# Hybrid decoder block on one core: one weight ring for three stages, adaLN columns run on, and two of eight one-hot units made by ScalarE

## Chip, cores and metric

One core of one Trainium2 chip. The metric is device microseconds of one execution, the median of the runs. Engines are named as in the profile: PE is TensorE (PEld its weight loads), DVE is VectorE, ACT is ScalarE, POOL is GpSimd, SP is SyncE, which issues most DMA transfers.

## The reference, cut to what matters

One sequence of T = 512 positions, width D = 1024, all in float32. adaLN: a vector c gives six vectors of shift, scale and gate.

```python
mod = jax.nn.silu(c) @ w_ada[l] + b_ada[l]            # 1024 x 6144
sh1, sc1, gt1, sh2, sc2, gt2 = jnp.split(mod[:, None, :], 6, axis=-1)
h = rmsnorm(x, norm_pre_mix[l]) * (1.0 + sc1) + sh1
y = token_mixer(h, ...)
x = x + gt1 * rmsnorm(y, norm_post_mix[l])
h = rmsnorm(x, norm_pre_ffn[l]) * (1.0 + sc2) + sh2
y = peer(h, w_q[l], sub_keys[l], u_tab[l], v_tab[l])
x = x + gt2 * rmsnorm(y, norm_post_ffn[l])
```

The token mixer projects h by w_in, runs a gated short convolution and a gated delta rule (q and k normed by head, chunks of 64), and merges:

```python
merged = jax.nn.sigmoid(gate_sc) * br_sc + jax.nn.sigmoid(gate_dn) * br_dn
return merged @ w_mix_out
```

peer picks 16 of 16384 experts per head and position (8 heads) with gates from a softmax, and sums over them gate × gelu(h · u) × v:

```python
act = jax.nn.gelu(jnp.einsum('btd,bted->bte', hb, u), approximate=False)
return jnp.einsum('bte,bted->btd', gb * act, vv)
```

## The kernel before

Everything runs in float32 precision on TensorE by parts: a float32 tile is split into a high part in fp32r (a copy on ScalarE, "hi") and the rest (a subtraction, "lo"), and a product is three matmuls, hi × hi, lo × hi and hi × lo. A weight tile is 128x1024 (8 blocks of 128x128, 512 KB), so each tile costs a load on SyncE's queue, a split on ScalarE of about 1.06 us, a subtraction on GpSimd of about 2.33 us, and 24 matmuls of 512 columns.

The program is a row of stages, each one block in which every engine has its own instruction stream and waits for the others by semaphores. A helper (Steps) names the counts: V, A and E are the steps of VectorE, ScalarE and TensorE, and `V.after("lo3")` is the wait for VectorE's step lo3. A stage ends when all engines have ended.

*First stage (project_stage, 0 to 180 us).* c goes through Silu into the PSUM tile `bank_pair`, the same row in all partitions. The adaLN products are made by VectorE: for each of 48 columns of w_ada, transposed to a 128x1024 tile of the ring `ada` (6 buffers), one scalar_tensor_tensor with accumulator, L428. The first 16, shift and scale of the first norm, are needed for h; the other 32 lie between later work. For x, ScalarE squares (L364) and takes the root, VectorE inverts (L437) and scales x to `xn` (L440), TensorE transposes xn (L294), ScalarE applies scale and shift (h_raw, L380) and copies the high part (h_hi, L383), and VectorE subtracts (h_lo, L452). This goes in rounds k = 0, 2, 4, 6 of four columns and two tiles of h. TensorE multiplies each h tile by w_ab (L307), and then tile n of 16 of the projection (L318), whose weights pass through `wring` (4 buffers). Behind tile 11 it sums the squares of q and k by head and spreads the inverse norm (L337), for which ScalarE takes the root of a 16x512 tile and VectorE the reciprocal (L503), both in the slot n == 10 of their loops over tiles.

*Delta stage (180 to 407 us).* The delta rule of 8 chunks, and 12 further projection tiles between its parts.

*Merge stage (merge_stage, 408 to 617 us).* It has its own tiles merge_w, merge_w_hi and merge_w_lo of two buffers. First VectorE makes a gate vector and a diagonal 128x1024 tile twice (L1102, L1104); TensorE turns each into a row that all partitions hold (L996), and ScalarE copies it out. ScalarE copies the high parts of both branches, VectorE subtracts the low ones (L1108). Then four rounds of six weight pieces (two gates and one piece of both branches' outputs, twice): L1005, with the sigmoid on ScalarE and the products and sums on VectorE. At the end eight pieces of w_mix_out, k = 0 to 7, go into all eight PSUM banks, one per output (4 blocks of positions, 2 halves), L1028; for the last two pieces both are waited for and each output takes k = 6 and 7 together. ScalarE squares each output for the norm (L1086).

*Retrieve stage (617 to 1043 us).* The queries, the choice of experts, and products h · u for some of them. Its last steps turn the experts' row and column indices and the gates of 384 positions into `idxT` and `gateT`.

*Gate stage (scatter_stage, 1043 to 1306 us).* For each of the 384 positions, a 128x128 matrix of gates over all 16384 experts is made by a product of two one-hot matrices on TensorE: `hot1` (hot_i in the trace) compares a row of numbers with the first index, for eight positions in one operation of 128x1024 (L1588), and `hot2` (gated_i) compares it with the second index and multiplies by the gate, one operation of 128x128 for each position, with two pointers (L1592):

```python
last = nc.vector.tensor_scalar(hot2[:, u % RH, t, :], C["iota"], idxT[:, 1, at], gateT[:, at], ALU.is_equal, ALU.mult)
```

There are 6 iterations of 8 units of 8 positions. A unit is eight such products (16 matmuls in the trace, L1624); ScalarE copies them out of two PSUM banks in two pieces (L1652), and they are stored. PSUM has room for two units, the one-hots have four buffers (RH = 4). In six of the eight units (0, 1, 2, 4, 5, 6) TensorE also multiplies a tile of u by h (24 matmuls of 384 columns, L1633), whose split is on ScalarE (L1642), whose low part is on VectorE (L1597), and whose Gelu is on ScalarE (L1660). VectorE has one more product of 128x1024 per unit (L1601), for the 128 positions whose experts are gathered by row instead. VectorE, TensorE and ScalarE each run a hardware loop over the iterations.

*Expert stage (1307 to 1947 us).* The products h · u that are left, the gates times gelu, and the sum over v, in 128 tiles. The change touches it only by the buffer of its v tiles.

## Time and profile before

| | us |
|---|---|
| median of 3 runs | 1945.85 (1945.83 to 1947.31) |
| the profiled execution | 1948.68 |
| its span | 1946.8 |
| PE busy | 1786.5 (92%) |
| DVE busy | 1339.8 (69%) |
| ACT busy | 701.2 (36%) |
| POOL busy | 757.5 (39%) |
| mean granted TensorE clock | 0.965 of full |

The span is from the first to the last instruction of the profiled execution, which is one of its own and not one of the three. A busy share is a mean over stages of different kinds: what matters for a change in one stage is who waits for whom in that stage. TensorE's granted clock is 1.00 or 0.50 of full speed in a short stretch (2.4 and 1.2 GHz).

### The profile page before, as it was taken

The page shows a single profiled execution, that of the slowest core. Times are in us where ns is not written, and L with a number is a line of the kernel's source. Part 1 is how long each engine was busy: PE and PEld are TensorE (multiplying, and loading weights), DVE is VectorE, ACT ScalarE, POOL GpSimd, SP SyncE. Part 2 cuts the span into 40 slices and gives each one's busy share as a digit, 9 for nine tenths or more (in the row PEclk, how much of TensorE's full clock was granted, in tenths as well). Part 3 has the DMA queues.
Part 4 walks back from the last instruction along what each step waited for, and adds up shares of the span by engine and source line. Part 5 has one row for each costly group of instructions (what it writes and reads, how often), then busy time and mean ns, then how long its engine had stood idle before and what let it go on. Part 6 is the DMA issues. An engine that isn't in the chain of part 4 may idle for free. (4 is left out here: it accounts for less than half of the span.)

```text
span 1946.8 us, 31281 instructions
## 1 busy us (share of the span) xinstructions
PE 1786.5 (92%) x11421; PEld 1570.5 (81%) x11421; DVE 1339.8 (69%) x2857; ACT 701.2 (36%) x1041; POOL 757.5 (39%) x443
## 2 busy tenths in 40 slices
PE   2899899979995998999998999979999999999997
PEld 1566777868874787999998999969998888888886
DVE  4783555543323467878776999967787888777776
ACT  3432223333314323333333445433333333333333
POOL 0332233214432345777772333313455443333330
PEclk9898999989997999999998999989999999999999
DMA  7672010013322226888885999998789999988983
GB/s 256 228 256 87 24 35 13 2 55 97 97 87 101 73 87 205 291 291 285 290 280 173 304 313 302 312 315 287 262 326 331 360 370 368 328 322 317 327 319 114
DMA packets 178681, 432.51 MB, mean 222 GB/s; under 512 B 15752, under 2 KB 91656, under 8 KB 178464
## 3 DMA queue, kind: packets, MB, share of 16 engines
q1 hardware_dynamic: 125088, 273.71, 42.1%
q0 software_dynamic: 36864, 134.23, 19.2%
q10 hardware_dynamic: 16640, 23.36, 3.3%
q8 instruction: 57, 0.93, 0.2%
q14 instruction: 32, 0.26, 0.0%
HBM read 383.54 MB, written 47.71 MB: 222 GB/s over the span
## 5 line engine op out<-in xcount | busy, mean ns | idle before, releaser
L198 POOL DMA_INDIRECT own_rows<-in_peer_v_dram,own_row x128 | 214.4, 1675 | 328.7 <-DVE y_own L1888 310.0
L1384 POOL TENSOR_TENSOR piece_lo<-v_tile,piece_hi 128x1024 fp32r<-128x1024 f32 x84 | 202.0, 2405 | 153.8 <-ACT piece_hi L1314 153.7
L198 POOL DMA_INDIRECT own_rows<-in_u_rows_dram,own_row x128 | 161.8, 1264 | 246.9 <-DVE own_rows L1601 185.4
L1245 PE MATMUL bank<-h_hi,piece_hi 128*128 128x384 f32 (+1 forms) x672 | 237.2, 353 | 13.8 <-DVE h_lo L1490 7.0
L1245 PE MATMUL bank<-h_lo,piece_hi 128*128 128x384 f32 (+1 forms) x672 | 234.9, 350 | 0.0
L1245 PE MATMUL bank<-h_hi,piece_lo 128*128 128x384 f32 (+1 forms) x672 | 234.9, 350 | 0.0
L1798 PE MATMUL bank<-v_hi,coef_lo 128*128 128x512 f32 x512 | 199.7, 390 | 0.0
L1798 PE MATMUL bank<-v_lo,coef_hi 128*128 128x512 f32 x512 | 199.6, 390 | 0.0
L1798 PE MATMUL bank<-v_hi,coef_hi 128*128 128x512 f32 x512 | 199.2, 389 | 0.1
L1314 ACT ACTIVATE piece_hi<-v_tile 128x1024 fp32r<-128x1024 f32 x84 | 89.3, 1063 | 254.2 <-PE bank L1245 244.9
L1873 DVE TENSOR_TENSOR v_lo<-v_tile,v_hi 128x1024 fp32r<-128x1024 f32 x128 | 156.5, 1223 | 24.7 <-ACT v_hi L1829 22.8
L1888 DVE SCALAR_TENSOR_TENSOR y_own<-own_rows,own_coef,y_own 128x1024 f32<-128x1024 f32 x128 | 163.8, 1280 | 1.3 <-DMA own_rows<-in_peer_v_dram,own_row 0.2
L1829 ACT ACTIVATE v_hi<-v_tile 128x1024 fp32r<-128x1024 f32 x128 | 135.0, 1055 | 48.2 <-PE bank_pair L1798 48.2
L1245 PEld LDWEIGHTS bank<-h_hi,piece_hi 128*128 128x128 f32 x672 | 127.6, 190 | 21.4 <-issue 10.7
L1833 ACT ACTIVATE coef_hi<-coef 128x384 fp32r<-128x384 f32 x128 | 67.1, 524 | 211.5 <-DVE coef L1912 211.5
L1245 PEld LDWEIGHTS bank<-h_hi,piece_lo 128*128 128x128 f32 x672 | 127.3, 189 | 6.0
L1245 PEld LDWEIGHTS bank<-h_lo,piece_hi 128*128 128x128 f32 x672 | 127.5, 190 | 5.5
L1052 POOL TENSOR_TENSOR merge_w_lo<-merge_w,merge_w_hi 128x1024 fp32r<-128x1024 f32 x32 | 76.4, 2388 | 141.6 <-ACT merge_w_hi L1059 141.6
L1531 DVE SCALAR_TENSOR_TENSOR own_rows<-own_rows,bank_pair 128x1024 f32<-128x1024 f32 x64 | 77.8, 1216 | 52.0 <-DMA own_rows<-in_u_rows_dram,own_row 51.8
L1798 PEld LDWEIGHTS bank<-v_hi,coef_lo 128*128 128x128 f32 x512 | 96.1, 188 | 20.1
L1798 PEld LDWEIGHTS bank<-v_hi,coef_hi 128*128 128x128 f32 x512 | 96.1, 188 | 19.8 <-issue 0.5
L1798 PEld LDWEIGHTS bank<-v_lo,coef_hi 128*128 128x128 f32 x512 | 96.1, 188 | 19.5
(399 smaller groups left out, 4255.8 us busy)
## 6 DMA issues: line engine op xcount, KB each, us to landing
v_tile<-in_peer_v_dram SPq DMA_DIRECT2D x128, 512.0 KB, 5.3
v_tile<-in_peer_u_dram SPq DMA_DIRECT2D x68, 512.0 KB, 4.8
ada<-in_w_ada_dram SPq DMA_DIRECT2D x48, 512.0 KB, 5.2
gate_scratch<-gate_block SPq DMA_DIRECT2D x48, 512.0 KB, 6.5
gate_tiles<-gate_scratch SPq DMA_DIRECT2D x32, 768.0 KB, 6.8
gelu_scratch<-gelu_early ACTq DMA_DIRECT2D x104, 192.0 KB, 4.6
gelu<-gelu_scratch SPq DMA_DIRECT2D x104, 192.0 KB, 5.3
u_early<-in_peer_u_dram SPq DMA_DIRECT2D x36, 512.0 KB, 5.4
```

What stands on the lines that cost most here:

```text
L198: pool.indirect_dma_start(own_rows[:, n % R], None, tables[n // NS], bass.IndirectOffsetOnAxis(ap=own_row[:, n % NS:n % NS + 1], axis=0)). ...
L1052: nc.gpsimd.tensor_tensor(w_lo[:, b], wm[:, b], w_hi[:, b].bitcast(F32), ALU.subtract).then_inc(lo_ready, 1)
L1245: last = nc.tensor.matmul(out, ww[:, n % HR, k, :], x[:, k, 0:nt], start=(k == 0 and m == 0), stop=(k == KT - 1 and m == 2))
L1314: nc.scalar.activation(w_hi[:, n % HR], w[:, n % WR], ACT.Copy).then_inc(hi_ready, 1)
L1384: nc.gpsimd.tensor_tensor(w_lo[:, n % HR], w[:, n % WR], w_hi[:, n % HR].bitcast(F32), ALU.subtract).then_inc(lo_ready, 1)
L1531: nc.vector.scalar_tensor_tensor(rows[:, i % R], rows[:, i % R], 1.0, h_psum[:], ALU.mult, ALU.mult, accum_out=own_act[:, bass.ds(n, 1)]). ...
L1798: last = nc.tensor.matmul(y_bank(t, half)[:], w[:, j, t * P:(t + 1) * P], x[:, j, c], start=(first and n == 0), stop=(final and n == 2))
L1829: nc.scalar.activation(v_hi[:, e % G], vt[:, e % G], ACT.Copy).then_inc(v_hi_ready, 1)
L1833: nc.scalar.activation(c_hi[:, e % G], coef[:, e % 2], ACT.Copy).then_inc(c_hi_ready, 1)
L1873: return nc.vector.tensor_tensor(dst, src, hi.bitcast(F32), ALU.subtract)
L1888: nc.vector.scalar_tensor_tensor(y_own[:], rows[:, n % R], own_coef[:, n - NS:n - NS + 1], y_own[:], ALU.mult, ALU.add).then_inc(row_used, 1)
```

## The change

Five things are changed.

1. *Start of the first stage.* h_lo is made by GpSimd with a semaphore of its own, and no longer by VectorE. VectorE does columns 4 and 5 ahead of 1/std and xn, and the others behind them without a wait for h. The ring `ada` has 8 buffers. The loads on ScalarE's queue stand in another order, six small ones behind Silu, and each block of x has its own semaphore. Three tiles lie in memory of others (h_raw and the squares in scT, sel16 in row_ffn).
2. *The norm of q and k.* Root and reciprocal stand in the slot n == 9 instead of n == 10.
3. *One weight ring.* `weight_ring` of four buffers holds the projection's tiles, the merge pieces and later the v tiles. SyncE loads merge pieces 0 to 3 in the delta stage, and ScalarE and GpSimd split pieces 0 and 1 there. TensorE does pieces 0 and 1 ahead of the diagonal rows. The loops over merge rounds of TensorE and ScalarE are written out.
4. *The last two pieces of w_mix_out.* k = 6 for all eight outputs, then k = 7.
5. *Gate stage.* In units 3 and 7 of each iteration VectorE makes hot1 alone. ScalarE makes hot2 for these two: |column number − index| by Abs with a pointer as bias, and Relu(gate − gate × distance), with gateT and neg_gateT as pointers, eight of each, ahead of the copy of the unit two before. neg_gateT is one operation more at the end of the retrieve stage. ScalarE's loop over the iterations is written out.

```diff
+        ring = sb(top, "weight_ring", [P, WRING, D])
...
+            env["v_tile"] = ring
...
-    AR, K2 = 6, 2
+    AR, K2 = 8, 2
...
             def _(pool):
                 pool.wait_ge(ab_hi, 1)
                 nc.gpsimd.tensor_tensor(wab_lo, w_ab[:], wab_hi.bitcast(F32), ALU.subtract).then_inc(ab_lo, 1)
-                for n in range(N_HERE + 2):
+                def rest(n):
                     pool.wait_ge(hi_ready, n + 1)
                     nc.gpsimd.tensor_tensor(w_lo[:, n % 2], wring[:, n % WRING], w_hi[:, n % 2].bitcast(F32), ALU.subtract).then_inc(lo_ready, 1)
+
+                for k in range(KT):
+                    pool.wait_ge(*A.after(f"hi{k}"))
+                    nc.gpsimd.tensor_tensor(h_lo[:, k, :], h_raw[:, k % 2], h_hi[:, k, :].bitcast(F32), ALU.subtract).then_inc(h_low, 1)
+                    if k == KT - 3:
+                        rest(0)
+                for n in range(1, N_HERE + 2):
+                    rest(n)
...
                     if k == KT - 3:
                         split(0)
-                    if k == KT - 2:
+                    if k == KT - 1:
                         split(1)
...
-                    if n == 10:
+                    if n == 9:
                         act.wait_ge(ss_done, 8)
                         nc.scalar.activation(nrm[:], ss_ps[0:2 * H, :], ACT.Sqrt, bias=eps[0:2 * H]).then_inc(norm_done, 1)
...
                     for n in range(2 * k, 2 * k + 2 * K2):
                         mod_column(n)
+                        if n == 5:
+                            dve.wait_ge(*A.after("std"))
+                            nc.vector.reciprocal(stat[:, 2, :], stat[:, 1, :]).then_inc(*V.step("rstd"))
+                            dve.wait_ge(*V.after("rstd"))
+                            for t in range(TT):
+                                nc.vector.tensor_scalar(xn[:, t * D:(t + 1) * D], x_tok[:, t, :], stat[:, 2, t:t + 1], None, ALU.mult).then_inc(*V.step(f"xn{t}"))
...
-                    for j in range(k, k + K2):
-                        dve.wait_ge(*A.after(f"hi{j}"))
-                        nc.vector.tensor_tensor(h_lo[:, j, :], h_raw[:, j % 2], h_hi[:, j, :].bitcast(F32), ALU.subtract).then_inc(*V.step(f"lo{j}"))
...
-                    if n == 10:
+                    if n == 9:
                         dve.wait_ge(norm_done, 1)
                         nc.vector.reciprocal(nrm[:], nrm[:]).then_inc(inv_done, 1)
...
-                for n in range(N0 + WRING, N_PROJ):
+                for n in range(N0 + WRING, N_PROJ + WRING):
                     sp.wait_ge(lo_ready, n - WRING + 1)
-                    sp.dma_start(wring[:, n % WRING], a["w_proj"][n]).then_inc(s_w[n % WRING], 16)
+                    sp.dma_start(wring[:, n % WRING], a["w_proj"][n] if n < N_PROJ else a["w_merge"][n - N_PROJ]).then_inc(s_w[n % WRING], 16)
...
+                            if i == 0 and m == 1:
+                                rows()
...
-                pe.wait_ge(lo_ready, NW)
-                for t, half in outs:
-                    mix(KT - 2, 0, t, half, False, False)
-                    mix(KT - 1, 1, t, half, False, True).then_inc(*E2.step(f"y{half}_{t}"))
...
+                nc.vector.tensor_scalar(g_["neg_gateT"][:], bank[4][:, 0:TD], -1.0, None, ALU.mult).then_inc(*VP.step("neg_gT"))
...
+        by_act = (3, 7)
...
+                def one_hot(i, u):
+                    n = i * len(by_act) + by_act.index(u)
+                    act.wait_ge(*(E.after(f"unit{u - RH}", i) if u >= RH else E.after(f"unit{NU + u - RH}", i, 1)))
+                    for t in range(UT):
+                        at = i * (NU * UT) + u * UT + t
+                        last = nc.scalar.activation(hot2[:, u % RH, t, :], C["iota"], ACT.Abs, bias=idxT[:, 1, at:at + 1], scale=-1.0)
+                    last.then_inc(far, 1)
+                    act.wait_ge(far, n + 1)
+                    for t in range(UT):
+                        at = i * (NU * UT) + u * UT + t
+                        last = nc.scalar.activation(hot2[:, u % RH, t, :], hot2[:, u % RH, t, :], ACT.Relu, bias=gateT[:, at:at + 1], scale=neg_gateT[:, at:at + 1])
+                    last.then_inc(hot_act, 1)
...
                     for u in range(NU):
                         slot = u // UB
+                        if u + 2 in by_act:
+                            one_hot(i, u + 2)
```

Three places show how instructions move. The first is VectorE at the start of the first stage. The rows of before are the first of its four rounds, its columns (L428), the vectors and the h_lo tiles behind them, and the second round's columns:

```order
L428 SCALAR_TENSOR_TENSOR ada,mod<-ada,bank_pair 128x1024 x4
L437 RECIPROCAL stat<-stat 128x4
L440 TENSOR_SCALAR xn<-x_tok,stat 128x1024 x4
L444 TENSOR_TENSOR mod<-mod,b_ada 128x2
L445 TENSOR_TENSOR mod<-mod,b_ada 128x2
L447 TENSOR_SCALAR scale<-mod 128x2
L449 TENSOR_TENSOR scale<-scale,norms 128x2
L452 TENSOR_TENSOR h_lo<-h_raw,h_hi 128x512 x2
L428 SCALAR_TENSOR_TENSOR ada,mod<-ada,bank_pair 128x1024 x4
```

The same place of the kernel after the change:

```order
L442 SCALAR_TENSOR_TENSOR ada,mod<-ada,bank_pair 128x1024 x4
L459 TENSOR_TENSOR mod<-mod,b_ada 128x2
L460 TENSOR_TENSOR mod<-mod,b_ada 128x2
L462 TENSOR_SCALAR scale<-mod 128x2
L464 TENSOR_TENSOR scale<-scale,norms 128x2
L442 SCALAR_TENSOR_TENSOR ada,mod<-ada,bank_pair 128x1024 x2
L451 RECIPROCAL stat<-stat 128x4
L454 TENSOR_SCALAR xn<-x_tok,stat 128x1024 x4
L442 SCALAR_TENSOR_TENSOR ada,mod<-ada,bank_pair 128x1024 x2
```

The first scale and shift and two more columns have moved ahead of the reciprocal and xn, and h_lo is gone from VectorE. It stands on GpSimd now, with the low part of the first projection tile between the sixth and the seventh:

```order
L353 TENSOR_TENSOR h_lo<-scT,h_hi 128x512 x6
L349 TENSOR_TENSOR wring_lo<-weight_ring,wring_hi 128x1024
L353 TENSOR_TENSOR h_lo<-scT,h_hi 128x512 x2
L349 TENSOR_TENSOR wring_lo<-weight_ring,wring_hi 128x1024 x17
```

The second place is ScalarE in the gate stage. Before, the loop's first units: the copies of a unit's gates (L1652), the split of a u tile (L1642), its Gelu (L1660), and two table loads in the loop's body:

```order
L1652 ACT_TABLE_LOAD
L1652 ACTIVATE gate_block<-bank 128x128x4 x2
L1656 ISA
L1641 ISA
L1642 ACTIVATE u_early_hi<-u_early 128x1024
L1659 ISA
L1660 ACT_TABLE_LOAD
L1660 ACTIVATE gelu_early<-bank 128x384
```

After (L1696, L1671 and L1704 are the same three, L1678 and L1683 are Abs and Relu):

```order
L1696 ACTIVATE gate_block<-bank 128x128x4 x2
L1671 ACTIVATE u_early_hi<-u_early 128x1024
L1704 ACT_TABLE_LOAD
L1704 ACTIVATE gelu_early<-bank 128x384
L1706 DMA gelu_scratch<-gelu_early 128x384
L1678 ACTIVATE gated_i<-cst,idxT 128x128 x8
L1683 ACTIVATE gated_i<-gated_i,gateT,neg_gateT 128x128 x8
L1696 ACTIVATE gate_block<-bank 128x128x4 x2
L1671 ACTIVATE u_early_hi<-u_early 128x1024
L1704 ACTIVATE gelu_early<-bank 128x384
L1706 DMA gelu_scratch<-gelu_early 128x384
```

The sixteen activations for unit 3 stand between unit 0's Gelu and unit 1's copies, and one table load is left in the stage.

The third place is TensorE at the start of the merge stage: the diagonal rows (L996), the loop's branch, and the first of the 24 matmuls of the first piece. Before:

```order
L996 MATMUL bank<-diag,cst 128x128 x8
L996 MATMUL bank_pair<-diag,cst 128x128 x8
L1008 UNCONDITIONAL_BRANCH
L1008 ISA
L1016 ISA
L1005 MATMUL bank<-h_hi,merge_w_hi 128x512
L1005 MATMUL bank<-h_lo,merge_w_hi 128x512
L1005 MATMUL bank<-h_hi,merge_w_lo 128x512
```

After, at the boundary of pieces 1 and 2 (L1015 is the products' line now, L1005 the diagonal rows'):

```order
L1015 MATMUL bank<-h_hi,wring_hi 128x512
L1015 MATMUL bank<-h_lo,wring_hi 128x512
L1015 MATMUL bank<-h_hi,wring_lo 128x512
L1005 MATMUL bank<-diag,cst 128x128 x8
L1005 MATMUL bank_pair<-diag,cst 128x128 x8
L1015 MATMUL bank<-branches_hi,wring_hi 128x512
L1015 MATMUL bank<-branches_lo,wring_hi 128x512
L1015 MATMUL bank<-branches_hi,wring_lo 128x512
```

The diagonal rows have moved from ahead of piece 0 to between pieces 1 and 2; the loop's branch is gone.

## Rows read from the trace of the kernel before

**Rows 1.** TensorE's waits in the span: total us, times, longest us.

```profile
PE bank L294 <- DVE mod L445: 27.4, 1, 27.4
PE bank L307 <- DVE h_lo L452: 17.7, 4, 5.9
PE bank L1624 <- DVE gated_i L1592: 12.4, 11, 4.5
PE bank L1028 <- POOL merge_w_lo L1052: 3.6, 1, 3.6
```

**Rows 2.** Timeline 18 to 62 us: start, us, engine, what, [idle, releaser].

```profile
18.39 1.06 ACT L364 ACTIVATE xn<-x_tok 128x1024 f32<-128x1024 f32 x1 [9.57 <-DMA x_tok<-in_x_dram]
...
24.51 2.74 DVE L440 TENSOR_SCALAR xn<-x_tok,stat 128x1024 f32<-128x1024 f32 x4
...
37.35 0.78 ACT L380 ACTIVATE h_raw<-bank,mod,scale 128x512 f32<-128x512 f32 x1 [5.99 <-DVE scale L449]
...
41.90 1.22 DVE L428 SCALAR_TENSOR_TENSOR ada<-ada,bank_pair 128x1024 f32<-128x1024 f32 x1
43.04 1.22 DVE L428 SCALAR_TENSOR_TENSOR ada<-ada,bank_pair 128x1024 f32<-128x1024 f32 x1
...
61.59 0.63 PE L318 MATMUL bank<-h_hi,wring_hi 128*128 128x512 f32 x1
```

**Rows 3.** DMA view, 0 to 70 us in 40 slices of 1.75 us.

```profile
GB/s 0 239 404 406 311 389 326 308 394 410 412 410 410 407 131 0 0 0 0 77 293 309 379 140 98 281 309 337 382 400 417 337 377 309 94 368 344 152 9 0
```

**Rows 4.** Timeline from 138 us; a window: busy by engine, granted clock, DMA.

```profile
138.66 3.33 DVE L503 RECIPROCAL norm<-norm 16x512 f32<-16x512 f32 x1
...
142.05 3.78 PE L337 MATMUL bank<-norm,sel 16*128 16x512 f32 x4 [3.23 <-DVE norm L503]
...
143.00:145.00 2.00, 2.00 (x4) 0.66 (x2) 1.93 (x4) 0.00 (x0) 0.00 (x0) 0.50 0.84 238
...
152.89 1.98 PE L337 MATMUL bank<-norm,sel 16*128 16x512 f32 x4
...
160.51 1.98 PE L337 MATMUL bank<-norm,sel 16*128 16x512 f32 x4
```

**Rows 5.** Timeline of the merge stage's start, 407 to 440 us.

```profile
407.87 1.23 DVE L1104 TENSOR_TENSOR diag<-cst,gate 128x1024 f32<-128x1024 f32 x1
...
412.24 4.66 POOL L1052 TENSOR_TENSOR merge_w_lo<-merge_w,merge_w_hi 128x1024 fp32r<-128x1024 f32 x2 [36.09 <-ACT merge_w_hi L1059]
...
414.65 3.33 DVE L1104 TENSOR_TENSOR diag<-cst,gate 128x1024 f32<-128x1024 f32 x1
417.91 2.28 DVE L1108 TENSOR_TENSOR branches_lo<-scT,branches_hi 128x2048 fp32r<-128x2048 f32 x1
...
422.59 0.49 PE L1005 MATMUL bank<-h_hi,merge_w_hi 128*128 128x512 f32 x1 [0.77 <-DVEq L1110]
...
439.25 1.28 DVE L1117 TENSOR_TENSOR merge_work<-merge_work,bank 128x512 f32<-128x512 f32 x2 [16.86 <-PE bank L1005]
```

**Rows 6.** Timeline of the merge stage's end.

```profile
599.64 0.60 ACT L1086 ACTIVATE merge_work<-bank 128x512 f32<-128x512 f32 x1 [1.78 <-PE bank L1028]
```

**Rows 7.** Gate stage: timeline of 1144 to 1160 us, and two windows.

```profile
1144.94 2.13 DVE L1592 TENSOR_SCALAR gated_i<-cst,idxT,gateT 128x128 f32<-128x128 f32 x8
...
1151.45 2.05 PE L1624 MATMUL bank<-gated_i,hot_i 128*128 128x128 f32 x16 [0.82 <-DVE gated_i L1592]
...
1157.53 1.95 PE L1624 MATMUL bank<-gated_i,hot_i 128*128 128x128 f32 x16
...
1159.23 0.42 PE L1633 MATMUL bank<-h_hi,u_early_hi 128*128 128x384 f32 x1
...
1163.48 1.95 PE L1624 MATMUL bank<-gated_i,hot_i 128*128 128x128 f32 x16
...
1050.00:1256.00 206.00, 198.13 (x1353) 196.23 (x1353) 206.00 (x468) 98.81 (x150) 67.44 (x40) 1.00 0.94 296
1256.00:1306.00 50.00, 38.98 (x268) 38.60 (x266) 37.42 (x85) 15.31 (x26) 12.76 (x8) 0.93 0.99 338
```

183 lines of the change are left out of this document (96 added, 87 removed).

## The prediction

> **What bounds the kernel now.** I read the page first: TensorE is busy 92% of the span and VectorE 69%, and the chain that ended last is one stretch of 32% of the span, TensorE in the expert stage, which the change leaves alone. So whatever the change brings comes from places where TensorE waits before that, and I took the view of waits for TensorE next [rows 1]. The reader is to see four lines there that the change touches: 27.4 us before the first transpose of the first stage and 17.7 us in four pieces behind it, 3.6 us for the last merge weight, and eleven waits of 12.4 us in all in the gate stage; a fifth, 3.23 us for a reciprocal, stands in its row's brackets [rows 4]. The timeline of each place, the DMA view of the first 70 us and two stretches of the gate stage [rows 2 to 7] say what each wait costs and what comes due when it is gone.
>
> **Start of the first stage.** Before, VectorE does four adaLN columns, scale and shift, then waits for ScalarE's h to make two h_lo tiles, and only then the next four columns: four rounds. The first w_proj product starts at 61.59 [rows 2]. After, h_lo is on GpSimd and VectorE never waits for ScalarE. The last of x lands as before, when the first square started, at 18.39. But the three squares ahead no longer wait for it: std, there at 24.3 before (VectorE's inversion follows it, and xn at 24.51 [rows 2]), comes three squares of 1.0 sooner, at 21.3. VectorE is at columns 4 and 5 until about 22.2, which I take from the arrival of their weights; then inversion and four xn of 2.74 [rows 2] end at 25.2. Ten columns are left; one costs 1.14 start to start (41.90 to 43.04 [rows 2]): 11.4, and three groups of four small ones at about 0.8 (0.15 to 0.17 each, and a restart): 2.3. So the last scale is there at 25.2 + 13.7 = 38.9, if the columns' weights are. They come at about 1.3 us for 512 KB at the 400 GB/s of the full slices [rows 3]; eight buffers instead of six let SyncE run ahead, and the sixteenth lands at about 34. The last two h, each 0.78 and a copy of about 0.60 [rows 2, 6], end at about 41.8. GpSimd's h_lo of 128x512 isn't in the trace. From below it is half of the 128x1024 one (4.66 for two, so 1.17 [rows 5]), from above all of it, 2.33; a fixed part of a tenth makes 1.25, and I take that. The last h_lo is then due at 43.3, the first product at 44.7 after the small w_ab products, and about 0.9 is lost since TensorE runs at half clock longer: **−16.0** (13 to 18; 10 if the columns wait for weights).
>
> **The norm.** Tile 11 ends at 138.8, but the spreading product waits for VectorE's reciprocal of 3.33, and after the idle time four of them take 3.78 against 1.98 later, at a granted clock of 0.50 in 143 to 145 [rows 4]. 138.8 to 152.89 is 14.1 against 7.62 for the same work one tile on (152.89 to 160.51 [rows 4]): 6.5 lost. With square root and reciprocal one tile earlier, the reciprocal is done some 3 us before it is wanted; the convolution of the tile behind it comes 3.3 us later and has a tile's slack. Two small waits of about 0.1: **−6.3** (5 to 6.6).
>
> **Merge start.** Before, the first product is at 422.59, since two weights are loaded, split and subtracted only then, and GpSimd's two subtractions (412.24 to 416.9) run beside VectorE's second gate and diag: the diag takes 3.33 against 1.23 for the same operation undisturbed, the gate 1.65 [rows 5]. The third piece ends at 439.25. After, pieces 0 and 1 are ready as the stage begins. TensorE does them from 408.2 to about 421.7 (before, the three pieces took 439.1 − 422.6 = 16.5, so 5.5 each; 11.0 for two, and 2.5 for a start at half clock after idle time), then the diag rows that came ahead of them before, then piece 2. What is late next: GpSimd's subtraction for piece 3 waits for piece 1, so it starts at about 422.9, when VectorE wants the second diag (it waits for the first rows, as before). I take the same stretching as in the row: diag to 426.5, rows to 428.5, two br_lo of 2.28 less their overlap with that to 431.0, piece 2 from there, 5.5 and 2.4 for another slow start: 438.9. The delta stage ends about 0.5 later for two more splits and subtractions in it, which is in these times. **−0.3**, between +3 and −5.
>
> The Trainium skill (VectorE: DVE Perf Modes, Two Vector instructions with no wait between them) says that an operation with two SBUF inputs reads the second through an interface that it shares with GpSimd. The trace agrees, with 3.33 against 1.23 us; it would put the subtraction and the diag in each other's way again, and leaves the small gain above rather than the 4.5 us of the second rival below.
>
> **Merge tail.** TensorE waits 3.6 for the last weight's low part [rows 1], and restarts at half clock; the second half-output's square is at 599.64 [rows 6]. After, it does the eight outputs' products with k = 6 in that time and ends each with k = 7: the same square is at 597.5. What follows runs on ScalarE and VectorE in the same steps: **−2.1** (1.5 to 2.6).
>
> **Gate stage.** VectorE is busy in all 206 us of 1050 to 1256, TensorE in 198.1 [rows 7]. One of its units costs, in starts, 1.14 for the first one-hot, 2.05 for eight gated ones (2.13 with the overlap [rows 7]), 1.15 for the own rows' product and in six of eight units 1.13 for a low part: 6 × 5.47 + 2 × 4.34 = 41.5 per iteration. TensorE needs 5.95 for a unit with a tile's product (1157.53 to 1163.48) and 1.70 for one without (1157.53 to 1159.23, where the product starts [rows 7]): 6 × 5.95 + 2 × 1.70 = 39.1. So it waits 0.82 twice per iteration [rows 1, 7], and each wait costs 2.77 − 1.70 in starts (0.82 and 1.95 against 1.70) and 0.1 in the restart, about 1.2. Of the eleven the first, 4.5 at the stage's start, stays, nine are of 0.82 or 0.83, and one is of 0.36: 9 × 1.2 + 0.7 = 11.5. After, VectorE leaves the gated one-hots of two units to ScalarE: 41.5 − 4.1 = 37.4, under TensorE's 39.1, and the waits should go. From the 11.5 I take 1.2 for the last iteration, where 50 us have TensorE busy only 38.98 and DMA at 0.99 already [rows 7], and 0.5 for the new negation ahead of the stage: **−9.5** (4 to 11.5).
>
> ScalarE's price: sixteen activations of 128x128 per unit. The nearest rows are 0.60 for 128x512 without pointers [rows 6] and 0.78 with two [rows 2]; 1.06 for 128x1024 [rows 2]. From 0.60 and 1.06 a straight line gives 0.14 + 0.12 = 0.26 at 128 columns, and a pointer costs 0.09. So 0.31 to 0.44 each, 3.7 to 5.9 a unit; bounds are 0 below and 0.78 above, 12.5 a unit. They stand ahead of the copy of the unit two before, which TensorE wants for unit 3 (or 7): 5.95 × 2 less the copies (2.1) and the split (1.1) leave 8.7, that is 0.54 for each. Up to that they cost nothing, since ScalarE is busy 98.8 of 206 us [rows 7]; the work that hides them is TensorE's tile product. The loop written out removes two table loads per iteration (before, both stood in it).
>
> The Trainium skill (ScalarE: Activation LUTs, What ACT_TABLE_LOAD costs) gives 280 ns + 0.833 ns per column with a pointer as bias, 93 more for a further one and 93 less back to back: an estimate of 8 × 0.29 + 8 × 0.39 = 5.5 us a unit, inside the slack. The same page (Rules for kernel authors) sends relu and multiply to VectorE, not ScalarE; here VectorE is the full engine (206.00 of 206.00), and by that rule alone the forecast would be the last rival's.
>
> **The sum.** 16.0 + 6.3 + 0.3 + 2.1 + 9.5 = 34.2. It is made against the profiled execution, 1948.68 with a span of 1946.8; the median of the runs is 1945.85, 2.8 lower, with nothing in the profile to set it apart. 1945.85 − 34.2 = 1911.6; I say **1911.5** (the profiled one 1914.5). A measurement here tells about 0.2%, 3.9 us, from no change.
>
> **Rivals.**
> *DMA takes over in the gate stage.* The transfers are at share 0.94 and 296 GB/s in 1050 to 1256, and 0.99 and 338 in 1256 to 1306 [rows 7]. The same bytes in 39.1 instead of 41.5 need 314 GB/s, near 1.0 of share. For it: the share is near full. Against: 338 is above 314, and no tile waits for a load before 1256. The stage gains 0 to 5: 1917 to 1921. Chance 0.2.
> *No collision at the merge start.* If GpSimd's subtraction comes before or after the second diag, this takes 1.23 and piece 2 ends at about 434.5: 1907. Chance 0.15.
> *adaLN weights bind the start.* Slices of 308 to 326 GB/s among those of 400 [rows 3] mean the columns may not come every 1.3 us, and they queue behind the new order of small loads: gain 10, 1917.5. Chance 0.1.
> *ScalarE is too slow, and the kernel slower.* With c for one activation, each of twelve units costs 16c − 8.7 on TensorE's path. The other parts bring 24.7, so the kernel is slower from 12 × (16c − 8.7) > 24.7, c = 0.67. Only pointer activations of 128 columns that cost nearly what 512 do (0.78) would reach it: then 12 × 3.8 = 45 lost against 24.7, 1966. Chance 0.02.
>
> **How the numbers follow.** The forecast has 0.5; its own range is 1907 to 1916. With the first rival and the third together on the high side (both come to 1924) and on the low side the second with a start of 18 and a gate stage of 11.5 (1903), 0.8 of the chance lies in **1903 to 1924**; the rest is mostly beyond 1924, where two parts fail at once. All cases but the last are faster by over 0.2%: **faster 0.96, same 0.02, slower 0.02**.
>
> **What would show it.** The first w_proj product at 45 to 46 and no VectorE wait for h_hi in the first 45 us; no wait before the spreading product at about 123, and four of them in about 2.0; the second diag stretched to over 3 us beside GpSimd, and piece 2 done some 23 us before its old place (the shift of the stages before and 0.3); 3.6 us gone before the last outputs; no waits for gated one-hots but the first, a period of 39.1 in the gate stage, sixteen activations in 4 to 6 us and no table load there. The prediction is wrong if the period stays above 40 with waits for loads in it, if activations of 128 columns take over 0.54, or if the columns of the first stage wait for their weights.

## The result, and the profile after

The changed kernel takes 1915.45 us (median of 4 runs, 1914.6 to 1919.28) against 1946.58 for the kernel before (4 runs, 1945.83 to 1951.69): 31.1 us less, a ratio of 0.9838 with a 95% interval of 0.9817 to 0.986. It is faster, by 3.1 us less than the 34.2 that were forecast, and inside the range; the time is 4.0 above the 1911.5 of the forecast. The profiled execution took 1919.28, with a span of 1917.4, 29.4 under the span before; it is the longest of the four, and its delta stage is also the longest of all profiles in the table below.

TensorE's waits in the span, as in [rows 1]: total us, times, longest us.

```profile
PE bank L298 <- DVE xn L454: 25.4, 1, 25.4
...
PE bank L311 <- POOL h_lo L353: 6.9, 3, 4.1
PE bank L1653 <- DVE gated_i L1619: 5.0, 1, 5.0
...
PE bank_pair L1005 <- DVE diag L1125: 3.1, 1, 3.1
...
PE bank L1653 <- ACT gate_block L1696: 2.6, 1, 2.6
```

The four waits of [rows 1] are to be read against these. The one ahead of the first transpose is 25.4 instead of 27.4. The one for the last merge weight is gone. h_lo is waited for 6.9 us instead of 17.7 (on GpSimd now). For gated one-hots only the stage's first wait is left, 5.0. The wait for ScalarE's copy in the gate stage is 2.6, and was 1.4 before; the 3.1 for the second diagonal was 5.1.

The timeline of the first 47 us of the changed kernel, which answers to [rows 2]:

```profile
19.89 1.22 DVE L442 SCALAR_TENSOR_TENSOR ada<-ada,bank_pair 128x1024 f32<-128x1024 f32 x1 [1.71 <-DMA ada<-in_w_ada_dram]
...
31.02 1.29 POOL L353 TENSOR_TENSOR h_lo<-scT,h_hi 128x512 fp32r<-128x512 f32 x1 [0.30 <-ACT h_hi L397]
...
32.80 0.86 DVE L459 TENSOR_TENSOR mod<-mod,b_ada 128x2 f32<-128x2 f32 x1
...
38.26 2.36 POOL L349 TENSOR_TENSOR wring_lo<-weight_ring,wring_hi 128x1024 fp32r<-128x1024 f32 x1
...
38.74 1.91 DVE L459 TENSOR_TENSOR mod<-mod,b_ada 128x2 f32<-128x2 f32 x1
...
41.15 0.78 ACT L394 ACTIVATE scT<-bank,mod,scale 128x512 f32<-128x512 f32 x1 [3.26 <-DVE scale L464]
...
42.67 1.27 POOL L353 TENSOR_TENSOR h_lo<-scT,h_hi 128x512 fp32r<-128x512 f32 x1 [2.04 <-ACT h_hi L397]
...
46.63 0.63 PE L322 MATMUL bank<-h_hi,wring_hi 128*128 128x512 f32 x1
```

The first projection product has come from 61.59 to 46.63. On the way to it two of VectorE's small sums of 128x2 last 0.86 and 1.91 where 0.15 is normal, and each ends within 0.04 us of the end of a GpSimd subtraction: 32.80 + 0.86 = 33.66 with 33.65, where two h_lo of 2.63 together end that began at 31.02, and 38.74 + 1.91 = 40.65 with 38.26 + 2.36 = 40.62. ScalarE's h waits for the scale behind it (41.15).

The spreading products of the norm, which answer to [rows 4]:

```profile
123.14 1.12 PE L341 MATMUL bank<-norm,row_ffn 16*128 16x512 f32 x2
...
130.97 0.69 PE L341 MATMUL bank<-norm,row_ffn 16*128 16x512 f32 x1 [0.17 <-DVE qkvT L490]
...
140.17 1.98 PE L341 MATMUL bank<-norm,row_ffn 16*128 16x512 f32 x4
```

The first is not waited for and takes 1.98. The third comes 9.20 behind the second, not 7.6: in 133 to 135 the granted clock is 0.65, though nothing is waited for there.

The merge stage, at its start and at its end, which answers to [rows 5] and [rows 6]:

```profile
391.50 0.17 DVE L1123 TENSOR_TENSOR gate<-mod,norms 128x8 f32<-128x8 f32 x1 [0.81 <-PEq L619]
...
406.13 2.34 POOL L1063 TENSOR_TENSOR wring_lo<-weight_ring,wring_hi 128x1024 fp32r<-128x1024 f32 x1 [3.04 <-ACT wring_hi L1077]
406.78 1.71 DVE L1123 TENSOR_TENSOR gate<-mod,norms 128x8 f32<-128x8 f32 x1 [13.85 <-PE bank L1005]
408.52 1.23 DVE L1125 TENSOR_TENSOR diag<-cst,gate 128x1024 f32<-128x1024 f32 x1
...
409.81 3.57 PE L1005 MATMUL bank_pair<-diag,cst 128*128 128x128 f32 x16 [3.07 <-DVE diag L1125]
...
414.30 0.47 PE L1015 MATMUL bank<-branches_hi,wring_hi 128*128 128x512 f32 x1 [0.92 <-DVEq L1131]
...
414.30:420.00 5.70, 5.70 (x25) 4.72 (x26) 0.00 (x0) 0.00 (x0) 0.00 (x0) 1.00 0.01 3
...
420.06 0.69 DVE L1138 TENSOR_TENSOR merge_work<-merge_work,bank 128x512 f32<-128x512 f32 x1 [5.90 <-PE bank L1015]
...
421.19 2.39 POOL L1063 TENSOR_TENSOR wring_lo<-weight_ring,wring_hi 128x1024 fp32r<-128x1024 f32 x1 [12.73 <-ACT wring_hi L1077]
421.38 2.76 DVE L1140 TENSOR_TENSOR merge_work<-merge_work 128x512 f32<-128x512 f32 x1
...
578.44 0.60 ACT L1107 ACTIVATE merge_work<-bank 128x512 f32<-128x512 f32 x1
```

The line of 414.30 to 420.00 is a window, with columns as in [rows 7]. Here the diagonal takes its normal 1.23, and it is the gate vector ahead of it that waits, 1.71, until GpSimd's operation ends (408.49 and 408.47). Piece 2 starts at 414.30 and runs at a granted clock of 1.00. The first merged product (L1138, 420.06) stands 28.6 behind the stage's first operation (391.50), and 31.6 before.

ScalarE's sixteen activations in the gate stage, the copies behind them, and the one wait of TensorE for a copy:

```profile
1073.59 2.46 ACT L1678 ACTIVATE gated_i<-cst,idxT 128x128 f32<-128x128 f32 x8 [0.40 <-PE bank L1653]
1076.08 3.19 ACT L1683 ACTIVATE gated_i<-gated_i,gateT,neg_gateT 128x128 f32<-128x128 f32 x8
1079.18 1.06 ACT L1696 ACTIVATE gate_block<-bank 128x512 f32<-128x512 f32 x2
...
1245.04 2.62 PE L1653 MATMUL bank<-gated_i,hot_i 128*128 128x128 f32 x16 [2.63 <-ACT gate_block L1696]
```

Eight Abs take 2.46 and eight Relu 3.19, 5.65 together (5.59 from the first start to that of the copy behind them). The window of 140 us in the same stage (columns as in [rows 7]: busy us of PE, PEld, DVE, ACT and POOL with counts, granted clock, DMA share, GB/s):

```profile
1060.00:1200.00 140.00, 140.00 (x969) 140.00 (x969) 135.88 (x283) 100.68 (x215) 48.66 (x29) 1.00 0.97 329
```

TensorE is busy throughout (before, 134.6 of the same 140 us), VectorE no longer is, and DMA moves 329 GB/s.

### The profile page after: what moved, and what is told of

Read it like the earlier page. It is cut to its first block and busy times, and to the rows that moved or that the text cites. A ratio compares the mean times of both kernels' runs of the same rounds, so it can differ in the third digit from the quotient of the medians.

```text
span 1917.4 us, 30996 instructions
## 1 busy us (share of the span) xinstructions
PE 1782.5 (93%) x11421; PEld 1572.1 (82%) x11421; DVE 1312.8 (68%) x2754; ACT 744.9 (39%) x1217; POOL 766.1 (40%) x451
## 5 line engine op out<-in xcount | busy, mean ns | idle before, releaser
L1405 POOL TENSOR_TENSOR piece_lo<-weight_ring,piece_hi 128x1024 fp32r<-128x1024 f32 x84 | 202.1, 2406 | 150.3 <-ACT piece_hi L1335 150.3
L1335 ACT ACTIVATE piece_hi<-weight_ring 128x1024 fp32r<-128x1024 f32 x84 | 89.3, 1063 | 252.9 <-PE bank L1266 245.0
L1916 DVE TENSOR_TENSOR v_lo<-weight_ring,v_hi 128x1024 fp32r<-128x1024 f32 x128 | 156.6, 1223 | 24.4 <-ACT v_hi L1872 22.4
L1872 ACT ACTIVATE v_hi<-weight_ring 128x1024 fp32r<-128x1024 f32 x128 | 135.0, 1055 | 48.2 <-PE bank_pair L1841 48.2
L1063 POOL TENSOR_TENSOR wring_lo<-weight_ring,wring_hi 128x1024 fp32r<-128x1024 f32 x30 | 71.7, 2391 | 112.3 <-ACT wring_hi L1077 112.3
```

Of the source, the lines that this page charges most:

```text
L1063: nc.gpsimd.tensor_tensor(w_lo[:, b % 2], wring[:, b], w_hi[:, b % 2].bitcast(F32), ALU.subtract).then_inc(lo_ready, 1)
L1335: nc.scalar.activation(w_hi[:, n % HR], w[:, n % WR], ACT.Copy).then_inc(hi_ready, 1)
L1405: nc.gpsimd.tensor_tensor(w_lo[:, n % HR], w[:, n % WR], w_hi[:, n % HR].bitcast(F32), ALU.subtract).then_inc(lo_ready, 1)
L1872: nc.scalar.activation(v_hi[:, e % G], vt[:, e % G], ACT.Copy).then_inc(v_hi_ready, 1)
L1916: return nc.vector.tensor_tensor(dst, src, hi.bitcast(F32), ALU.subtract)
```

## Experiments

All are edits of the changed kernel, but for the last. The table sets the stages side by side, in us of each profile: to the first projection product; from there to the delta stage's first product; the delta stage; the merge stage up to its first merged product; the rest of it; the retrieve stage up to the first one-hot product; from there to the expert stage's first product; what is left; the span; and the median of all runs of that kernel.

| | first | to delta | delta | merge start | merge rest | retrieve | gate | expert | span | median |
|---|---|---|---|---|---|---|---|---|---|---|
| before | 61.6 | 118.9 | 227.2 | 31.6 | 177.9 | 429.4 | 262.6 | 637.6 | 1946.8 | 1946.6 |
| before_again | 61.7 | 119.2 | 224.0 | 31.8 | 178.6 | 428.4 | 262.1 | 637.8 | 1943.7 | (one run) |
| after | 46.6 | 113.5 | 231.4 | 28.6 | 175.9 | 428.8 | 254.6 | 638.0 | 1917.4 | 1915.45 |
| g_none | 46.6 | 113.9 | 228.2 | 28.6 | 175.9 | 428.8 | 262.4 | 637.5 | 1922.1 | 1923.2 |
| g_seven | 46.5 | 113.5 | 228.1 | 28.5 | 175.9 | 427.3 | 257.2 | 637.5 | 1914.4 | 1918.1 |
| g_abs2 | 46.7 | 113.2 | 230.8 | 28.7 | 176.0 | 428.8 | 262.3 | 637.6 | 1924.0 | 1926.2 |
| g_abs3 | 46.7 | 113.8 | 228.3 | 28.5 | 175.9 | 426.9 | 290.5 | 638.3 | 1949.0 | 1950.9 |
| n_late | 46.6 | 117.9 | 224.4 | 27.8 | 177.1 | 427.0 | 255.4 | 637.4 | 1913.8 | 1918.5 |
| s_ring6 | 47.0 | 113.3 | 228.0 | 28.5 | 175.8 | 428.8 | 255.7 | 637.4 | 1914.6 | 1916.1 |
| s_rest0 | 45.9 | 114.0 | 228.2 | 28.6 | 175.9 | 428.9 | 254.9 | 637.8 | 1914.2 | 1915.4 |
| s_pointer | 48.0 | 113.9 | 228.2 | 28.6 | 175.9 | 427.3 | 254.0 | 637.5 | 1913.4 | 1914.3 |
| s_fused | 45.0 | 113.9 | 228.2 | 28.6 | 175.9 | 428.3 | 255.7 | 638.2 | 1913.8 | 1914.95 |
| m_apart | 46.8 | 113.7 | 231.2 | 22.7 | 177.2 | 426.7 | 254.8 | 638.0 | 1911.0 | 1911.65 |
| best | 45.2 | 113.6 | 228.1 | 22.6 | 177.1 | 428.5 | 254.1 | 637.4 | 1906.7 | 1908.45 |

Where a stage's code is the same, it differs by some 3.4 us in the delta stage, 2.2 in retrieve, 1.7 in the gate stage and 1.4 in the merge rest. So an edit of 1 or 2 us is read from its own column, not from the median. The experiments were measured in three groups, and the kernel before took 1946.36 beside those named g, 1948.07 beside n_late, s_ring6, s_pointer and m_apart, and 1947.96 beside s_rest0, s_fused and best (1946.58 beside the changed kernel); the ratios allow for this, the medians do not.

### g_none: VectorE makes all one-hots

```diff
-        by_act = (3, 7)
+        by_act = ()
```

> The changed kernel with VectorE making all gated one-hots again; ScalarE's loop stays written out and the negation stays. If the relief of VectorE is what shortened the gate stage, the waits of 0.82 come back twice per iteration, the stage from its first to its last one-hot product goes from 239.8 back to about 248, and the time rises from 1915.5 by 8 to about 1923.5. If the gain came from the written-out loop and its missing table loads, the stage stays at 240 and the time at 1915.5.

Measured: 1923.21 us, ratio to the kernel before 0.9879 (0.9862 to 0.9895), 7.8 more than the changed kernel. Its waits and its window:

```profile
PE bank L1653 <- DVE gated_i L1619: 13.0, 11, 5.0
```

```profile
1060.00:1200.00 140.00, 134.14 (x918) 132.81 (x917) 140.00 (x320) 58.03 (x94) 45.36 (x27) 1.00 0.97 306
```

The eleven waits are back, VectorE is full again, and the gate column has its 262.4 of before. The written-out loop, without table loads, brings nothing of its own: before had 262.6 and 262.1 with them.

### g_seven: ScalarE makes those of unit 7 alone

```diff
-        by_act = (3, 7)
+        by_act = (7,)
```

> ScalarE makes the gated one-hots of unit 7 alone. VectorE then needs 41.5 - 2.05 = 39.45 per iteration, TensorE 39.25. If VectorE's total is what bound the stage, one unit is nearly enough: 0.2 per iteration lost, stage about 241, time 1916 to 1917. If it matters where in the iteration the relief comes, the wait before unit 4 stays: 6 x 1.1 more, 1922.

Measured: 1918.08 us (1913.65 to 1920.15), ratio 0.985 (0.983 to 0.987); the interval doesn't part it from the changed kernel.

```profile
PE bank L1653 <- DVE gated_i L1619: 5.0, 1, 5.0
...
PE bank L1653 <- ACT gate_block L1696: 3.5, 1, 3.5
```

```profile
1060.00:1200.00 140.00, 140.00 (x972) 139.62 (x971) 140.00 (x308) 78.45 (x149) 47.11 (x28) 1.00 0.98 322
```

In the steady part one unit is enough: no wait for a one-hot is left but the first, though VectorE has no idle time. So it is VectorE's total that bound the stage, not the place of the relief. The gate column is 2.6 above the changed kernel's, of which 0.9 is the longer wait for a copy in the last iteration (3.5 against 2.6). The rest is in the five iterations before it: the first takes 41.8 instead of 40.8 us from its first one-hot product to the next one's, and the other four 39.4 each instead of 39.25, close to the 39.45 that was expected from VectorE's total.

### g_abs2 and g_abs3: ScalarE's price raised

```diff
-                    for t in range(UT):
-                        at = i * (NU * UT) + u * UT + t
-                        last = nc.scalar.activation(hot2[:, u % RH, t, :], C["iota"], ACT.Abs, bias=idxT[:, 1, at:at + 1], scale=-1.0)
-                    last.then_inc(far, 1)
-                    act.wait_ge(far, n + 1)
+                    for again in range(2):
+                        for t in range(UT):
+                            at = i * (NU * UT) + u * UT + t
+                            last = nc.scalar.activation(hot2[:, u % RH, t, :], C["iota"], ACT.Abs, bias=idxT[:, 1, at:at + 1], scale=-1.0)
+                        last.then_inc(far, 1)
+                        act.wait_ge(far, n * 2 + again + 1)
```

In g_abs3 both twos are threes. The second and third pass write what the first wrote.

> ScalarE's eight Abs are made twice over, for both units of each iteration: 5.65 + 2.5 = about 8.1 a unit (the second pass writes the same values). By the slack of 8.7 in the prediction this costs nothing: 1915.5. By the trace of the changed kernel, in which the next unit's copies come out of this only 1.9 before TensorE wants them, 0.6 a unit plus the restart of a wait, some 0.5 to 1.5 each: 1922 to 1933.

> The eight Abs three times over: about 10.7 a unit. By the slack of 8.7: 2.0 x 12 = 24 longer, about 1940. By the slack of 7.5 that the trace of the changed kernel shows: 3.2 x 12 = 38 longer, about 1954. It also tells whether ScalarE's price is linear on TensorE's path, as the fourth rival assumed.

Measured: g_abs2 1926.2 us, ratio 0.9892 (0.9875 to 0.9908); g_abs3 1950.9 in its one run. TensorE's waits for copies in each, and g_abs3's activations:

```profile
PE bank L1653 <- ACT gate_block L1697: 7.3, 12, 3.4
```

```profile
PE bank L1653 <- ACT gate_block L1697: 30.1, 21, 3.2
```

```profile
1100.76 7.42 ACT L1679 ACTIVATE gated_i<-cst,idxT 128x128 f32<-128x128 f32 x24 [0.40 <-PE bank L1653]
1108.21 3.19 ACT L1684 ACTIVATE gated_i<-gated_i,gateT,neg_gateT 128x128 f32<-128x128 f32 x8
```

Against 254.6, the gate column is 7.7 longer at 5.65 + 2.48 = 8.1 a unit, and 35.9 at 10.6: 0.64 and 2.99 for each of the twelve units. The line through these two points has a slope of 0.95 and meets zero at 7.5. By it the slack is 7.5, not 8.7, and beyond it the price falls on TensorE nearly in full. With 10.6 a unit the whole gain of the change is gone (1950.9 against 1946.6), which is the fourth rival's mechanism; the changed kernel stands 1.8 a unit from its edge.

### n_late: the norm's slot undone

```diff
-                    if n == 9:
+                    if n == 10:
```

This in two places, ScalarE's root and VectorE's reciprocal.

> The changed kernel with root and reciprocal back in slot 10. The wait of 3.2 before the spreading product and the half clock behind it come back: from the first projection product to the delta stage's first product 118.9 instead of 113.2 to 113.9, the time 5 to 6 us more, about 1921. If the change of the slot only moved a stretch of half clock to another place, less than 3 us.

Measured: 1918.46 us (1914.0 to 1924.99), ratio 0.9856 (0.9827 to 0.9884), 3.0 more than the changed kernel; the intervals overlap, so the time alone does not part the two.

```profile
PE bank L341 <- DVE norm L515: 3.3, 1, 3.3
```

The wait is back, and the column to the delta stage is 4.4 longer. The delta column, whose code is the same, is 224.4, 3.6 or more below every other profile with the change. Both theories were half right: the place is worth 4.4 to 5.4, and some of it is given back behind it.

### s_ring6: six adaLN buffers

```diff
-    AR, K2 = 8, 2
+    AR, K2 = 6, 2
```

> The changed kernel with six adaLN buffers instead of eight. If the arrival of the columns' weights bound the first stage (the third rival), two buffers fewer put each later column behind by a transfer, and the first projection product comes 2 us or more later. If VectorE's own work binds it from column 6 on, as in the forecast, it stays at 46.6 to 47, and the time at 1915.5.

Measured: 1916.06 us, ratio 0.9835 (0.9819 to 0.9852). The first product comes at 47.0 instead of 46.6. So the two buffers more are worth 0.4 at most, and from column 6 on the weights bind nothing. Ahead of that they do: in the changed kernel VectorE waits 1.71 for the weights of column 4 (19.89), ends column 5 at 22.3, and only then inverts std, which is there at 21.4. That is up to 0.9 on the path, which six or eight buffers do not touch, and which the prediction carried.

### s_rest0: GpSimd's first subtraction of a projection tile moved back

```diff
-                    if k == KT - 3:
-                        rest(0)
-                for n in range(1, N_HERE + 2):
+                for n in range(N_HERE + 2):
                     rest(n)
```

> The changed kernel with GpSimd's low part of the first projection tile behind all eight h_lo instead of behind the sixth. If this subtraction is what makes VectorE's small sum last 1.91 at 38.7, it lasts 0.16 and the last scale is there 1.75 earlier; the low part is then ready at about 45.9 instead of 40.6, and the first projection product starts with it, at 46.0: 0.6 gained, not measurable in the time. If the sum waits for something else, it still lasts 1.9 and the first product comes at 47.7.

Measured: 1915.42 us, ratio 0.9825 (0.9802 to 0.9848).

```profile
38.76 0.16 DVE L457 TENSOR_TENSOR mod<-mod,b_ada 128x2 f32<-128x2 f32 x1
...
45.93 0.79 PE L322 MATMUL bank<-h_hi,wring_hi 128*128 128x512 f32 x1 [0.81 <-POOL wring_lo L349]
```

With nothing on GpSimd at 38.8 the sum takes 0.16, and the first product comes at 45.9 as forecast. The subtraction was the cause.

### s_pointer and s_fused: which forms wait for GpSimd

```diff
-                    nc.vector.tensor_tensor(mod[:, sc], mod[:, sc], b_ada[:, sc], ALU.add).then_inc(*V.step(f"scale_b{k}"))
+                    for j in range(K2):
+                        one = slice(SC1 + k + j, SC1 + k + j + 1)
+                        last = nc.vector.tensor_scalar(mod[:, one], mod[:, one], b_ada[:, one], None, ALU.add)
+                    last.then_inc(*V.step(f"scale_b{k}"))
```

The shift's sum and the scale's product are taken apart in the same way. In s_fused the sum with 1.0 goes too, and the line for the scale's sum is

```diff
+                        last = nc.vector.tensor_scalar(scale1[:, k + j:k + j + 1], mod[:, one], b_ada[:, one], 1.0, ALU.add, ALU.add)
```

> The changed kernel with the small sums and products of shift and scale of the first norm done column by column with a pointer as the second operand, so that no small operation has two SBUF tensors. In the changed kernel two of them last 0.86 and 1.91 instead of 0.16 beside GpSimd's subtractions. If the second SBUF operand is what waits for GpSimd, they last 0.1 to 0.2, the last scale comes 2 to 2.4 earlier less 0.3 for six more operations, and the first projection product starts at 44.7 to 45.0 instead of 46.6: 1913.7. If any VectorE operation waits for GpSimd, they stay long and nothing is gained.

> The changed kernel with shift and scale of the first norm made by operations of 128x1 with a pointer alone: two for the shift, two that add the bias and 1.0 at once, two for the product. In the run before, the 128x1 ones lasted 0.17 each even beside GpSimd's subtraction, and it was the 128x2 one with an immediate that lasted 1.21 and 1.29. If only these two forms (two SBUF tensors, and 128x2 with an immediate) wait for GpSimd, the second and third group take about 0.8 each instead of 1.25 and 2.3 in the changed kernel, and the first projection product starts at about 44.8 instead of 46.6: 1913.5. If whatever comes first beside GpSimd waits, it starts at 46.5 or later.

s_pointer: 1914.25 us, ratio 0.9839 (0.9808 to 0.987), and the first product at 48.0, 1.4 later than without it. The expectation failed. Its timeline:

```profile
28.29 1.21 DVE L468 TENSOR_SCALAR scale<-mod 128x2 f32<-128x2 f32 x1
...
39.74 2.35 POOL L349 TENSOR_TENSOR wring_lo<-weight_ring,wring_hi 128x1024 fp32r<-128x1024 f32 x1
...
40.47 0.33 DVE L465 TENSOR_SCALAR mod<-mod,b_ada 128x1 f32<-128x1 f32 x2
...
40.83 1.29 DVE L468 TENSOR_SCALAR scale<-mod 128x2 f32<-128x2 f32 x1
...
48.01 0.63 PE L322 MATMUL bank<-h_hi,wring_hi 128*128 128x512 f32 x1
```

The 128x1 operations with a pointer take 0.33 for two beside a GpSimd subtraction that runs from 39.74 to 42.09. But the 128x2 one with an immediate, which has one SBUF tensor alone, lasts 1.29 and ends at 42.12, with GpSimd's. So two SBUF tensors are not the only form that waits. s_fused: 1914.95 us, ratio 0.983 (0.9807 to 0.9854).

```profile
38.05 2.36 POOL L349 TENSOR_TENSOR wring_lo<-weight_ring,wring_hi 128x1024 fp32r<-128x1024 f32 x1
38.52 0.33 DVE L461 TENSOR_SCALAR mod<-mod,b_ada 128x1 f32<-128x1 f32 x2
...
39.14 0.34 DVE L470 TENSOR_SCALAR scale<-scale,norms 128x1 f32<-128x1 f32 x2
...
39.39 1.05 DVE L473 TENSOR_SCALAR neg_sel<-small 8x8 f32<-8x8 f32 x1
...
44.98 0.63 PE L322 MATMUL bank<-h_hi,wring_hi 128*128 128x512 f32 x1
```

With both forms gone from the chain the three pairs of 128x1 operations, shift, scale and product, run through beside GpSimd (38.05 to 40.41), and the first product is at 45.0, 1.65 earlier, close to the 44.8 that was expected. The next operation with an immediate, 8x8 at 39.39, waits 1.05 for the same subtraction, where nobody needs it.

### m_apart: the diagonal rows taken apart

```diff
                             last.then_inc(piece_done, 1)
-                            if i == 0 and m == 1:
-                                rows()
+                            if i == 0 and m < 2:
+                                rows(m)
...
-        pre_v = ["gate0", "diag0", "gate1", "diag1", "br_lo0", "br_lo1"]
+        pre_v = ["gate0", "diag0", "br_lo0", "br_lo1", "gate1", "diag1"]
```

> The changed kernel with the diagonal rows taken apart: the first two behind merge piece 0, the other two behind piece 1, and VectorE's two low parts of the branches ahead of its second gate and diagonal. If TensorE's wait of 3.1 for the second diagonal and its restart are what is left of the merge start, the wait goes, piece 2 follows at once, and the time from the stage's first operation to the first merged product falls from 28.6 to about 23: 5 to 6 us, 1910. If the second diagonal is pushed back by the two low parts or by GpSimd, it stays near 28.

Measured: 1911.65 us (1909.83 to 1912.89), ratio 0.981 (0.9793 to 0.9826).

```profile
401.00 2.39 POOL L1062 TENSOR_TENSOR wring_lo<-weight_ring,wring_hi 128x1024 fp32r<-128x1024 f32 x1 [9.70 <-ACT wring_hi L1076]
401.65 1.77 DVE L1125 TENSOR_TENSOR gate<-mod,norms 128x8 f32<-128x8 f32 x1 [3.58 <-PE bank L1004]
403.45 1.23 DVE L1127 TENSOR_TENSOR diag<-cst,gate 128x1024 f32<-128x1024 f32 x1
...
406.92 1.95 PE L1004 MATMUL bank_pair<-diag,cst 128*128 128x128 f32 x16
...
414.37 0.69 DVE L1137 TENSOR_TENSOR merge_work<-merge_work,bank 128x512 f32<-128x512 f32 x1 [9.70 <-PE bank L1014]
```

The gate vector waits for GpSimd once more (to 403.4), but the diagonal behind it is done at 404.7, over 2 us ahead of its need: TensorE has piece 1 in the meantime, does the second rows at 406.92 without a wait, and the merge start falls from 28.6 to 22.7. Of these 5.9 the merge rest gives back 1.3.

### best: both together

> The changed kernel with the diagonal rows taken apart as in the run that had it alone, and the 128x1 forms in the first stage. 5.9 less in the merge start, 1.2 of it given back in a stretch of half clock behind it as that run showed, and 1.8 less in the first stage if the forms are the cause: 1915.5 - 4.7 - 1.8 = 1909.0. If the forms bring nothing, 1911.

Measured: 1908.45 us (median of 5, 1905.43 to 1914.72), ratio to the kernel before 0.9801 (0.978 to 0.9823): 7.0 less than the changed kernel and 0.55 from what was expected. Both gains stand in their columns, 45.2 and 22.6. Its median is under those of s_fused and m_apart, but the interval overlaps that of m_apart.

### before_again: the kernel before, for a second profile

> The kernel before, unchanged, for a second profile. The delta stage took 227.2 in the first and 228.0 to 231.4 in seven of eight profiles with the change. If the two splits and subtractions that the change puts into it are what lengthens it by 2, it takes 227 again. If it is a matter of where stretches of half clock fall, whose steps of 1.6 its four parts show in every profile, it may as well take 229 to 231.

Measured: 1945.72 us. The delta stage takes 224.0, 3.2 less than in the first profile of the same kernel. The next section takes this up.

## Why the prediction was right, and where its terms were off

**The start** was forecast at −16.0 and brought 15.0. Up to xn each step came as said: std at 21.4, columns 4 and 5 until 22.3, xn done at 25.2, h_lo on GpSimd at 1.30 each (2.61 for two) for the 1.25 taken. The term that was off is "three groups of four small ones at about 0.8": they took 0.55, 1.25 and 2.3, 4.1 instead of 2.3, since two of the sums waited for GpSimd (s_rest0 and s_fused show it). So the first product came at 46.63, 1.9 later than the 44.7 of the sum and outside the 45 to 46 that were to show it. That the total is only 1.0 off is luck: the 0.9 that the sum took for a longer half clock was not lost, since the first tile took 6.24 us (46.63 to 52.87) and 6.42 before (61.59 to 68.01). No kernel was run with h_lo back on VectorE or with the columns back behind xn, so how the 15.0 divides between these two moves is read from the timeline and not shown; the same holds for the weight ring in the merge start. The collision that the prediction put into the merge stage also stood in the first stage, where the change itself had moved h_lo and a subtraction beside VectorE's small operations.

**The norm**, −6.3. The wait is gone and the products take 1.98, as forecast. The column to the delta stage is 5.4 shorter, and 4.4 by n_late. The two tiles about the place are 6.4 shorter together (15.27 instead of 21.64 us), so the term itself was right; what it had at nothing is that a stretch of half clock, 1.6 us long in its effect, now falls into the next tile.

**The merge start**, −0.3 with 0.5 lost in the stage ahead of it. The first merged product came 3.0 earlier within the stage. Counted from the stage's first operation, most steps came when the prediction's sum had them (its start is 408.2): pieces 0 and 1 took 13.3 (13.5), the second diagonal was done at 18.25 (18.3), and piece 2 began at 22.8 (22.8). The term that was off is the last, "5.5 and 2.4 for another slow start": piece 2 took 5.8, at a granted clock of 1.00 right behind diagonal rows at 0.54 on average (409.8 to 413.4). The kernel before had it already: there the diagonal rows ran at 0.50 (418.0 to 421.8), and the three pieces behind them at 1.00, 5.5 each.

The mechanism that failed is "I take the same stretching as in the row: diag to 426.5", though its end came out right. The row's 3.33 was read as the diagonal slowed throughout by GpSimd. The rows say something simpler: a VectorE operation of these forms waits for the end of the GpSimd operation that runs when it starts, and then takes about its normal time. Before, there were two GpSimd operations in a row, 412.24 to 416.90; the gate vector ended with the first (414.62) and the diagonal 1.08 after the second. After, there is one, and gate and diagonal take 2.97 together; the prediction had 3.6 with a start 0.6 earlier. The collision was there; its price was that of one wait, 1.5, on the gate vector and not on the diagonal, which took 1.23 instead of the "over 3 us" that were to show it. The time lies between the forecast and the second rival, but not by the rival's mechanism.

**The merge tail**, −2.1: the merge rest is 2.0 shorter in the profile. The square that stood 160.4 behind the first merged product (599.64) stands 158.4 behind it (578.44), and what follows takes 17.5 both times. No kernel was run with this edit undone, so that it is this edit is argued from that and the missing wait, not shown.

**The gate stage**, −9.5 forecast, 7.5 measured: 8.0 in its column and 0.5 lost to the negation (gates to the first one-hot product took 6.05 before and 6.52 after). g_none gives 7.8 for the relief alone. The period is 39.25, not 39.1: a unit without a tile's product takes 1.79 of TensorE, not 1.70, since 1.70 was read to the start of a product that overlaps; twelve such units make 1.1. The other part is the last iteration, where the wait for ScalarE's copy is 2.6 (1.41 before, a wait that the prediction did not carry); ahead of that copy ScalarE had waited 4.74 for a load. The prediction's own terms, 11.5 less 1.2 and 0.5, make 9.8, not 9.5. ScalarE's price was forecast at 3.7 to 5.9 and is 5.65; these bounds do not follow from the 0.31 to 0.44 for each activation that stand beside them, by which sixteen take 5.0 to 7.0, but the measured price lies in both. The Trainium skill (ScalarE: Activation LUTs, What ACT_TABLE_LOAD costs) gave an estimate of 5.5, and the trace agrees: 0.31 start to start with one pointer, 0.39 with two. The rule of the same page (Rules for kernel authors) that sends relu and multiply to VectorE is right here for one unit, which costs VectorE 2.05 and ScalarE 5.65; with VectorE full in [rows 7], following it would have given up the 7.8.

**The rivals.** DMA did not take over: 329 GB/s at a share of 0.97, without a wait for a load in the steady part. It shows only in the last iteration, where ScalarE waits 4.74 for a load. The adaLN weights did not bind from column 6 on (s_ring6). ScalarE has about 7.5 of slack, and its rival's mechanism is real from there on (g_abs2 and g_abs3).

**The delta stage** was forecast 0.5 longer, and is 4.2 longer in the pair of profiles (7.4 against before_again). In the three profiles with the norm's slot late (before, before_again, n_late) it takes 227.2, 224.0 and 224.4; in the eleven with it early 228.0 to 231.4. n_late has the two splits and subtractions that the change adds, so these are not the cause. The three intervals between ScalarE's roots for the four output norms in it each take one of four values in every profile, within 0.2: 52.7, 54.3, 55.8 or 57.4 us, in changing order, and the last is 52.7 to 52.9 in the three and 54.2 to 57.4 in the eleven. The granted clock was 0.84, 0.82, 0.94 and 0.94 in the four odd eighths of the stage before, and 0.81, 0.88, 0.86 and 0.94 in those of the changed kernel, so a part of the stage runs at half clock, and how much of it isn't the same each time. That the norm's slot does it is a correlation over fourteen profiles, three on one side; by what path stays open, and the kernel before alone differs by 3.2 between its two profiles. Whatever makes it gives back some of the norm's gain: n_late's median is only 3.0 above the changed kernel's.

**The sum** in the profiles: 15.0 + 5.4 − 4.2 + 3.0 + 2.0 + 0.6 (retrieve with the negation, code the same otherwise) + 8.0 − 0.4 (expert) = 29.4, the difference of the spans. That it is near the 34.2 is in part luck: the merge start brought 2.2 more than forecast, with its 0.5 counted, and the delta stage lost 3.7 more, and neither is a term that the prediction had right.

## What to carry to other kernels

When work moves to GpSimd, look at every small VectorE operation that can start while it runs: a 128x2 sum on the critical chain can cost as much as the rest of GpSimd's operation, and another form of the same sum may cost nothing. When one engine is full and another half idle, giving the idle one even a dearer form of the work pays, up to the slack of what is queued behind it; read that slack as the time from the last queued copy to its use, and raise the price in an experiment to see where it ends. A wait between two short steps on different engines (a diagonal, its rows, the next diagonal) can be filled with one of the long products that need neither (m_apart, 5.9).
